# Nine weight areas loaded in order of use, two gather buffers, an activation product in place

## The reference

```
def hier_moe(h, w_group, w_expert, w_gate, w_up, w_down):
    ...
    _, g_sel = lax.top_k(g_logit, 1)
    ...
    top_v, top_i = lax.top_k(e_sel, TOP_K_INNER)
    ...
    for g in range(N_GROUPS):
        hg = jax.nn.silu(jnp.einsum('td,edf->tef', t, w_gate[g])) * jnp.einsum('td,edf->tef', t, w_up[g])
        out = out + jnp.einsum('tef,efd->td', hg * comb[:, g, :, None], w_down[g])
```

## Time and profile before

| what | value |
|---|---|
| median of 3 runs | 1335.24 us (1334.73 to 1337.06) |
| profiled execution, its own time | 1332.0 us |
| its span | 1329.8 us |
| mean granted TensorE clock | 0.925 |
| TensorE busy | 1125.2 us (85%) |
| expert stage of layer 0, first gate-and-up product to last down product | 538.8 to 781.2 us |
| expert stage of layer 1, the same | 1057.5 to 1301.2 us |
| weights read per expert stage | 48 loads of 2048 KB |
| DMA rate in 600 to 770 us | 419 GB/s |

### The profile page before, as it was taken

One profiled execution on the slowest core, in us unless ns is written; L12 is line 12 of the kernel. 1 busy time (PEld: TensorE's weight loads), 2 busy tenths in 40 slices (PEclk: granted clock), 3 DMA queues, 4 the chain that ended last, 5 costly groups with the idle time before them and its releaser, 6 DMA issues.

```text
span 1329.8 us, 15315 instructions
## 1 busy us (share of the span) xinstructions
PE 1125.2 (85%) x6494; PEld 587.2 (44%) x6494; DVE 373.1 (28%) x854; ACT 246.4 (19%) x568; POOL 147.5 (11%) x135
## 2 busy tenths in 40 slices
PE   5999999999998996898777848997799599777871
PEld 3444444666897655333323314464345433223330
DVE  2511221234666423111101122019811311011114
ACT  4111211204301021111101112006611111011112
POOL 0000000143710000411110000000000221111000
PEclk9999999899999996898888888998899599888996
DMA  9210200000003535699999964015020699999955
GB/s 371 95 64 29 100 0 0 0 0 0 3 4 148 219 146 221 257 420 422 421 423 421 404 270 196 0 34 241 1 79 32 243 402 420 420 424 421 422 244 198
DMA packets 42235, 273.21 MB, mean 205 GB/s; under 512 B 8528, under 2 KB 9296, under 8 KB 21488
## 3 DMA queue, kind: packets, MB, share of 16 engines
q1 hardware_dynamic: 32368, 255.20, 46.8%
q0 software_dynamic: 9792, 16.94, 3.5%
HBM read 265.68 MB, written 23.21 MB: 217 GB/s over the span
## 4 chain that ended last, share of the span: by engine, by line
PE 62%; DMA 23%; DVE 8%; ACT 3%; issue 2%; SPq 0%; POOL 0%; DVEq 0%; POOLq 0%; ACTq 0%
DMA arena<-w_dn_dram 21%; PE bank L612 15%; PE bank L856 8%; PE bank L913 7%; PE bank L905 7%; PE bank L1030 5%; PE bank L692 4%; PE bank L653 2%; PE bank L660 2%; DVE arena L1747 2%; PE bank L596 1%; DVE arena L1717 1%; PE bank L944 1%; PE bank L555 1%; PE bank L847 1%
## 5 line engine op out<-in xcount | busy, mean ns | idle before, releaser
L905 PE MATMUL bank<-arena 128*64 128x512 f32 x1024 | 229.6, 601 | 1.7 <-ACT arena L1253 1.7
L913 PE MATMUL bank<-arena 128*64 128x512 f32 x512 | 140.0, 697 | 77.4 <-DMA arena<-w_dn_dram 70.4
L612 PE MATMUL bank<-arena 128*128 128x512 f32 x448 | 194.7, 594 | 0.9 <-ACT arena L1128 0.9
L905 PEld LDWEIGHTS bank<-arena 128*64 128x64 f32 x1024 | 81.5, 139 | 142.9 <-issue 140.2
L612 PEld LDWEIGHTS bank<-arena 128*128 128x128 f32 x448 | 84.8, 190 | 107.9 <-issue 106.8
L856 PE MATMUL bank<-arena 128*128 128x512 f32 x256 | 112.7, 595 | 0.7 <-ACT arena L1332 0.7
L913 PEld LDWEIGHTS bank<-arena 128*64 128x64 f32 x512 | 43.4, 159 | 152.7 <-issue 138.8
L1843 POOL DMA_INDIRECT arena<-h_dram,arena x32 | 32.7, 1022 | 437.2 <-DVE arena L1646 428.0
L1684 DVE COPY arena<-bank 128x512 f32<-128x512 f32 x32 | 22.1, 692 | 208.3 <-PE bank L913 208.3
L1847 POOL DMA_INDIRECT yk_dram<-arena x32 | 32.0, 999 | 398.2 <-DVE arena L1684 397.5
L1678 DVE TENSOR_TENSOR arena<-arena,bank 128x256 f32<-128x256 f32 x32 | 13.5, 421 | 215.3 <-ACT arena L1259 215.3
(11 more groups left out here) (234 smaller groups left out, 1163.4 us busy)
## 6 DMA issues: line engine op xcount, KB each, us to landing
arena<-w_gu_dram SPq DMA_DIRECT2D x52, 2048.0 KB, 28.3
arena<-w_dn_dram SPq DMA_DIRECT2D x32, 2048.0 KB, 26.5
arena<-w_in_dram SPq DMA_DIRECT2D x7, 2048.0 KB, 7.9
arena<-w_gu_dram SPq DMA_DIRECT2D x12, 1024.0 KB, 20.4
arena<-w_gu_dram SPq DMA_DIRECT2D x24, 512.0 KB, 25.2
arena<-w_out_dram SPq DMA_DIRECT2D x2, 4096.0 KB, 17.8
arena<-yk_dram SPq DMA_DIRECT2D x16, 512.0 KB, 6.9
arena<-w_qkv_dram SPq DMA_DIRECT2D x3, 2048.0 KB, 18.9
```

Source lines behind the costliest of these rows:

```text
L612: i = mm(pb[m % 4][:, :], wchunk[c % 3][:, k, (m % 4) * P:(m % 4 + 1) * P], HT[:, k, :], start=(k == 0), stop=(k == KT - 1))
L905: i = mm(out[cols, :], xT[:, k, cols], w(h, k), start=(k == 0), stop=(k == KT - 1))
L913: i = mm(pb[5 + c][cols, :], aT[:, f, cols], w[:, h, f, c * U:(c + 1) * U], start=(f == 0), stop=(f == 1))
```

## The change

It does five things.

- Down weights get a third area. Pair e uses set `e % 3` for its two gate and up pieces and its down weights, so there are nine areas. SP loads pair e+3's three pieces in order, each as soon as pair e's is read. Before the stage's first product all nine are loaded. The areas lie elsewhere: one gate-and-up piece of set 2 is now in four parts.
- The gather buffers `xg` go from four to two; a gather for pair e+2 waits until pair e is transposed, and the third and fourth gathers now stand between the table scatters.
- The product of silu and up is written over the silu (`act_h = sil`).
- The gain row for the norm behind the stage is loaded near the stage's end, not at its start. The first two attention projection pieces are loaded after the last down weights, once the down product of pair 13 is done.
- Between the layers, layer 1's first pair is loaded right after the last projection piece, and `wo[1]` waits until the query, key and value projections are done (`a_pm`), since it now lies where their weights were.

```diff
-        gu_piece = [[[(18 + 16 * j + 8 * c, 8)] for c in range(2)] for j in range(2)] + \
-                   [[[(78, 8)], [(74, 4), (92, 2), (98, 2)]]]
+        gu_piece = [[[(18, 8)], [(26, 8)]], [[(58, 8)], [(78, 8)]],
+                    [[(50, 8)], [(86, 3), (92, 1), (93, 1), (97, 3)]]]
...
-        dn = [units(50 + 8 * s, 8).rearrange("p (h f n) -> p h f n", h=2, f=FE // P) for s in range(2)]
+        dn = [units(a, 8).rearrange("p (h f n) -> p h f n", h=2, f=FE // P) for a in (34, 42, 70)]
...
-        xg = [units(66 + 2 * s, 2) for s in range(4)]
+        xg = [units(66 + 2 * s, 2) for s in range(2)]
...
-        act_h = [units(89)[:, 256 * s:256 * s + 256] for s in range(2)]
+        act_h = sil
...
-        def gu_turn(L, e):
-
-            j = (e + 2) % 3
-            return j, (NPAIR // 3 + (j == 2)) * L + e // 3 + 1
-
-        def dn_turn(L, e):
-
-            return (e + 1) % 2, NPAIR // 2 * L + e // 2 + 1
+        def turn_of(L, e):
+
+            j = e % 3
+            return j, len(range(j, NPAIR, 3)) * L + e // 3 + 1
...
-                sp.dma_start(GAIN[2 * L + 2], gains[2 * L + 2, :, :]).then_inc(ld_gain, 16)
+                load_down(L, 1)
+                load_gate_up(L, 2)
+                sp.wait_ge(s_tr, 8 * (2 * L + 2))
+                sp.wait_ge(r_hd, 16 * NT * (L + 1))
+                load_down(L, 2)
+
+                B = NPAIR * L
+                for e in range(NPAIR - 3):
+                    for c in range(2):
+                        sp.wait_ge(e_GU, 2 * (B + e) + 1 + c)
+                        load_gate_up(L, e + 3, (c,))
+                    sp.wait_ge(e_D, B + e + 1)
+                    load_down(L, e + 3)
                 if L == 0:
-                    load_gate_up(L, 0, (1,))
-                    load_gate_up(L, 2, (1,))
-                    load_down(L, 1)
-                else:
-                    load_gate_up(L, 0, (1,))
-                    load_gate_up(L, 2)
-
-                B = NPAIR * L
-                for e in range(NPAIR - 2):
-                    if e + 3 < NPAIR:
-                        for c in range(2):
-                            sp.wait_ge(e_GU, 2 * (B + e) + 1 + c)
-                            load_gate_up(L, e + 3, (c,))
-                    sp.wait_ge(e_D, B + e + 1)
-                    load_down(L, e + 2)
-                if L == 0:
+                    sp.wait_ge(e_D, NPAIR - 2)
                     for s in range(2):
                         sp.dma_start(aw[s], w_qkv[s, :, :, :]).then_inc(ld_wc[s], 16)
+                sp.wait_ge(e_GU, 2 * (B + NPAIR - 1))
+                sp.dma_start(GAIN[2 * L + 2], gains[2 * L + 2, :, :]).then_inc(ld_gain, 16)
...
             sp.wait_ge(c_o, 2)
+            load_gate_up(0, 0)
+            load_down(0, 0)
+            sp.wait_ge(o_n, NT)
             load_gate_up(0, 1)
-            load_gate_up(0, 2, (0,))
-            sp.wait_ge(o_n, NT)
-            load_down(0, 0)
-            load_gate_up(0, 0, (0,))
             moe_loads(0)
             sp.wait_ge(e_D, NPAIR)
             sp.dma_start(aw[2], w_qkv[2, :, :, :]).then_inc(ld_wc[2], 16)
+            sp.dma_start(negd, dconst[:, :].rearrange("p (b k) -> p b k", b=2)).then_inc(ld_dist, 16)
+            load_gate_up(1, 0)
+            load_down(1, 0)
+            sp.wait_ge(a_pm, 14)
             sp.dma_start(wo[1], w_out1[:, :, :]).then_inc(ld_wo, 16)
-            sp.dma_start(negd, dconst[:, :].rearrange("p (b k) -> p b k", b=2)).then_inc(ld_dist, 16)
-            sp.wait_ge(a_pm, 14)
-            load_gate_up(1, 1)
-            for e in range(2):
-                load_down(1, e)
+            load_gate_up(1, 1, (0,))
             sp.wait_ge(s_h, 3 * NT)
             routing_loads(1)
             sp.wait_ge(a_oc, 8)
-            load_gate_up(1, 0, (0,))
+            load_gate_up(1, 1, (1,))
             moe_loads(1)
...
+                def next_gather(e):
+                    pool.wait_ge(e_T, B + e - 1)
+                    gather(e, e % 2, gat_i[:, e:e + 1])
+
...
                 for e in range(NPAIR):
-                    if e + 4 < NPAIR:
-                        pool.wait_ge(e_T, B + e + 1)
-                        gather(e + 4, e % 4, gat_i[:, e + 4:e + 5])
+                    if 4 <= e + 3 < NPAIR:
+                        next_gather(e + 3)
```

More of the change, by code:

```diff
@@ L257, in trunk_program @@
         GAIN = [units(62, 2)] + [units(86, 2)] * 4
-        JUNK = [units(64, 2)] + [units(88, 2)] * 4
-        xg = [units(66 + 2 * s, 2) for s in range(4)]
+        JUNK = [units(64, 2)] + [units(89, 2)] * 4
+        xg = [units(66 + 2 * s, 2) for s in range(2)]
         xgT = [units(12 + 2 * s, 2).rearrange("p (k t) -> p k t", k=KT) for s in range(2)]
         yt = [units(8 + 2 * s, 2) for s in range(2)]
-        sil = [units(88)[:, 256 * s:256 * s + 256] for s in range(2)]
-        act_h = [units(89)[:, 256 * s:256 * s + 256] for s in range(2)]
+        sil = [units(89)[:, 256 * s:256 * s + 256] for s in range(2)]
+        act_h = sil
         actT = [units(90)[:, 256 * s:256 * s + 256].rearrange("p (j t) -> p j t", j=2) for s in range(2)]
@@ L279, in trunk_program @@
         GTEMP, BETA, GG, GC, KDS, KBS = range(6)
-        rt = units(94, 4)
+        rt = units(94, 3)
         lg = rt[:, 0:144].rearrange("p (t n) -> p t n", t=NT)
@@ L371, in trunk_program @@
         r_sc, r_hd = sem("ids_scattered"), sem("h_stored")
-        w_gs, w_ds = [sems(f"gate_up_loaded{j}_", 2) for j in range(3)], sems("down_loaded", 2)
-        def gu_turn(L, e):
-            j = (e + 2) % 3
-            return j, (NPAIR // 3 + (j == 2)) * L + e // 3 + 1
-        def dn_turn(L, e):
-            return (e + 1) % 2, NPAIR // 2 * L + e // 2 + 1
-        e_xg = sems("expert_gathered", 4)
+        w_gs, w_ds = [sems(f"gate_up_loaded{j}_", 2) for j in range(3)], sems("down_loaded", 3)
+        def turn_of(L, e):
+            j = e % 3
+            return j, len(range(j, NPAIR, 3)) * L + e // 3 + 1
+        e_xg = sems("expert_gathered", 2)
         e_T, e_xa, e_xd = sem("exp_transposed"), sem("exp_xT_a_copied"), sem("exp_xT_d_copied")
@@ L954, in gate_up @@
                     for c in range(2):
-                        b, turn = gu_turn(L, e)
+                        b, turn = turn_of(L, e)
                         pe.wait_ge(w_gs[b][c], 16 * len(gu_piece[b][c]) * turn)
@@ L971, in down @@
                         pe.wait_ge(e_yd, e + B)
-                    b, turn = dn_turn(L, e)
+                    b, turn = turn_of(L, e)
                     pe.wait_ge(w_ds[b], 16 * turn)
@@ L977, in moe @@
                 for e in range(NPAIR):
-                    gate_up(e, e % 4)
+                    gate_up(e, e % 2)
                     if e + 1 < NPAIR:
-                        transposes(e + 1, (e + 1) % 4)
-                    act_transposes(e, e % 4)
-                    down(e, e % 4)
+                        transposes(e + 1, (e + 1) % 2)
+                    act_transposes(e, e % 2)
+                    down(e, e % 2)
                     if e == 3:
@@ L1848, in scatter @@
                                           bounds_check=last_row, oob_is_err=False).then_inc(e_sc[j % 2], 16)
-                for j in range(4):
-                    gather(j, j, gat_i[:, j:j + 1])
+                def next_gather(e):
+                    pool.wait_ge(e_T, B + e - 1)
+                    gather(e, e % 2, gat_i[:, e:e + 1])
+                for e in range(2):
+                    gather(e, e, gat_i[:, e:e + 1])
                 pool.wait_ge(tab_init, 32)
```

29 lines of the change are left out of this document (15 added, 14 removed).

## The result

The changed kernel took 1320.07 us (median of 4 runs, 1317.84 to 1322.48), the kernel before on the same chip 1334.99 us (4 runs): a ratio of 0.9905, 95% interval 0.9882 to 0.9928. The forecast was 1317 us. The profiled execution had a span of 1319.6 us and a time of 1321.82 us at a mean clock of 0.941; before these were 1329.8, 1332.0 and 0.925.

The account below looks back on a forecast made before the run. DMA bytes were taken to set the expert stages' pace, 16.55 us a pair, so only the ends could gain: 7.7 us in layer 0 plus 10.7 in layer 1, 18.4 off 1335.2, gives 1317 us; bounds 1310 to 1329, range 1309 to 1328.

Parts of the forecast that it names:

- the two ends at which order can act: Expert stage's start (areas filled before the first release) and end (work behind the last weights); load order cannot change the pace between.
- sum of 18.4 us: Forecast gain of both layers together: 7.7 us in layer 0 and 10.7 us in layer 1.
- slot of 5.5: Time of one weight load in the full expert stage, 5.5 us, a pair's three loads taking 16.55 us.
- First gather: Stage start: the gather lands 0.2 us after the fuller queue empties, 1.9 us late in layer 0, 2.4 in layer 1.
- rival of a 7 us delay: Each stage's first gather waits 7 us, like gathers of the full stage, eating most of the gain: 1326 to 1332; chance 0.12.
- Ninth area: Stage start: one more load done before the first release, 39 instead of 40 follow, last weights land 5.5 us earlier per layer.
- Strict order: Stage end: pair 15's down weights land last, with only one down product behind them, taken as 4.5 us.
- End of layer 0: Two projection loads and the gain row (4.7 MB, 11.2 us) run against the last scatter, which lands at 778.4.
- Small edits: In the expert stages, two gather buffers for four and the product written in place were to cost nothing.
- Slower by the clock: Rival: after waits, each of a pair's three product bursts loses 2.9 us to half clock, 21.2 us a pair: 1381; chance 0.06.
- The waits vanish: Rival: loads stay ahead, both stages run at 12.5 us a pair, 70 us of waits go: about 1250; chance 0.03.

Follow-up runs that it names:

- changed again: The changed kernel without any edit, timed a second time: 1320.54 us, ratio 0.9907 to the kernel before.
- old order: Changed kernel, nine areas kept, but pair 14's down weights again issued behind pair 15's gate and up weights at each stage's end: 1333.08 us.
- projections behind the rows: Changed kernel with the first two attention projection loads issued after the read-back of the result rows: 1315.31 us.
- every piece split: Changed kernel with every gate-and-up piece loaded as four DMAs: 1325.88 us.
- new order alone: Kernel before, eight areas, with pair e+2's down weights issued ahead of pair e+3's gate and up weights from e = 6 on: 1321.66 us.
- the run with fewer bytes: Changed kernel loading only an eighth of each down-weight load from pair 3 on, so results are wrong: 1256.54 us, one run.
- small edits alone: Kernel before with two gather buffers, third and fourth gathers between the table scatters, and the product written over the silu: 1333.26 us.
- both moves: Changed kernel with the ninth load issued after the first gather lands and the two projection loads after the result rows' read-back: 1311.82 us, again 1313.40.

## Why the prediction was right, step by step

The bound, the two ends at which order can act, and the place of the new waits were as forecast: waits at gate and up pieces, from 648 us on (forecast 655), a pace of 16.5 us a pair, DMA share 1.01, one product behind the last weights, a last scatter over 4 us. The sum of 18.4 us was too large: the profiled span lost 10.2, the medians 12.5 to 15. That 1320.07 lies only 3 us above the forecast of 1317 is in part luck. In the traces 8 us of the sum are missing, and in the later runs 6: from their 1333.1 us for the kernel before, the same 18.4 us would have given 1314.7, against 1320.5. The terms:

| term | forecast, layers 0 and 1 | measured |
|---|---|---|
| first gather late | 1.9, 2.4 us | 3.0 (538.97 for 535.90), 3.5 (6.9 for 3.4) |
| refill: first issue to last weights | -4.9, -4.9 (a slot of 5.5, less 0.6) | -3.4 (222.3 for 225.7), -2.5 (222.8 for 225.3) |
| behind the last weights, to the last product's end | 4.5, 4.5 | 3.8, 5.5 |
| layer 0: last scatter lands behind the last weights | 11.4 | 11.8 |

- **First gather.** Mechanism right: it lands when the queue empties. In the four other kernels that were profiled with the whole ninth load ahead of both gathers (changed again, old order, projections behind the rows, every piece split) it landed 0.2 to 0.4 us behind that load in both layers too. Size off by 1.1 us in each layer: the queue emptied at 538.7 and not at 537.6, later than the load's 5.0 us less the gain row; why is open. The Trainium skill ("DMA: Bandwidth & Descriptors", section "Queues, rings and completion order") has DMA engines serve their queues in turn, packet by packet; by that alone the gather need not have waited for the queue to empty, and the traces show that it did (7.04 and 6.9 us for 4.10 and 3.4). The rival of a 7 us delay fell too.
- **Ninth area.** This is the term that was mis-sized most. I gave it a slot of 5.5 us less 0.6 for extra gathers. That counted one load less (2.10 MB) and took the other traffic as unchanged. The DMA queues from the first refill's issue to the last weights in layer 0 (packets, MB, share of 16 engines; q1 holds the plain loads, q0 the indirect transfers), after and then before, are

```profile
q1 hardware_dynamic: 10387, 84.76, 91.4%
q0 software_dynamic: 4096, 7.50, 8.9%
...
yk_dram<-arena POOLq DMA_INDIRECT x15, 10.0
arena<-h_dram,arena POOLq DMA_INDIRECT x13, 10.0
```

```profile
q1 hardware_dynamic: 10041, 86.22, 91.7%
q0 software_dynamic: 3872, 7.08, 8.2%
...
yk_dram<-arena POOLq DMA_INDIRECT x14, 10.3
arena<-h_dram,arena POOLq DMA_INDIRECT x12, 12.6
```

  The plain loads moved 1.46 MB less and not 2.10, because more of what stands behind the last weights in the queue moved before these had landed (2.97 MB for 2.33, by what is left when 39 and 40 weight loads are taken off). The gathers and scatters moved 0.42 MB more, with two more of them inside the refill. In layer 1 the same view (1063.1 to 1288.4 us before, 1062.4 to 1285.2 after) has 82.30 for 83.89 MB of plain loads and 7.63 for 7.14 of the others. There the gain row, of 0.52 MB, went from ahead of the stage to its end (issued at 1267.5, landed at 1286.3), and the forecast counted nothing for it there. Net, 1.04 and 1.10 MB less were moved, which at 420 GB/s is 2.5 and 2.6 us: by this estimate all of layer 1's 2.5 and most of layer 0's 3.4. In the traces the refills gave 5.9 us and the late gathers took 6.5 back; by the medians about 1 us was left, where 5.5 had been forecast (11.0 for two slots, less 4.3 for the gathers and 1.2 for the transfers). With the load out of the gather's way it was 4.7 us.
- **Strict order.** Right. The work behind the last weights shrank from 11.2 and 12.7 us to 3.8 and 5.5, 14.6 us together where 14.9 had been forecast. In whole kernels it was worth 11.0 us (the new order alone, with what it does to layer 0's last scatter in it) and 12.5 (the old order put back).
- **End of layer 0.** The number came out (11.8 us for 11.4), and the scatter did wait for the queue: it landed at 781.5, 0.2 us behind the gain row, the last of the loads ahead of it (issue, then landing):

```profile
L486 SPq DMA_DIRECT2D arena<-gains_dram x1: 328/328/328, 752.6 to 752.6; - x1
...
DMA to landing us min/median/max: 28.7/28.7/28.7
```

  But the working was not right, so the size was luck. The 11.2 us were 4.7 MB at the full rate. More than half of these had moved when the last weights landed at 769.7; behind that the engines moved 1.9 MB in 10 us, at 246 and 142 GB/s (last three numbers: granted clock, DMA share, GB/s):

```profile
770.00:775.00 5.00, 3.46 (x16) 1.04 (x13) 0.69 (x1) 0.90 (x2) 0.05 (x1) 1.00 0.60 246
775.00:780.00 5.00, 0.00 (x0) 0.00 (x0) 0.00 (x0) 0.98 (x1) 0.92 (x1) 0.77 0.36 142
```

  The slow end of the queue took the time, and not the bytes. That the projection loads cost about 3 us there is confirmed by moving them.
- **Small edits.** Nothing, as forecast.
- **Slower by the clock.** Fell as a loss, but not wholly. The granted clock over 600 to 770 us rose from 0.90 to 1.00, and in layer 0 every product that followed a wait for weights ran at 3.65 or 3.66 us a half. In layer 1 three of the 15 ran at 5.35 us, after 2.01, 2.50 and 1.21 us:

```profile
1231.36 5.35 PE L899 MATMUL bank<-arena 128*64 128x512 f32 x16 [2.50 <-DMA arena<-w_gu_dram]
```

  Two of them stood in a stage that waits for its loads anyway. The third is the last product, where its 1.7 us count: it is why 5.5 us passed behind layer 1's last weights. The Trainium skill ("TensorE: Matmul & The Clock Gate", section "HAM oscillation — how this bites in real kernels") describes a kernel in which every DMA wait, of some 3 to 5 us, sends the next burst off at half rate. The waits here were shorter, 0.5 to 2.8 us, and three of 34 had such an effect; so the loop that this rival took over for each burst did not come about.
- **The waits vanish.** Not with this change; the run with fewer bytes shows what it would take.

## What to carry to other kernels

Where a stage streams its weights at the DMA engines' full rate, count what work stands behind the last load to land: here one load two places too late at the end of each stage cost 11 to 12.5 us, while the bigger buffer gave about one in the changed kernel and nothing with the old order. The deeper prefetch paid only once the extra load no longer stood ahead of a small transfer that the stage's start waits for; issue it behind that. Bulk loads for the next stage did better behind the small last transfers of this one than ahead of them, by about 3 us here. Count, too, every transfer that a change moves into a stage whose pace is set by bytes, even a row of 0.5 MB.

## What the runs showed of the hardware

- Waits of one length did not always have one effect on the clock. The granted clock over 600 to 770 us was 0.90 with ten waits of up to 6.5 us (before), 0.91 with ten of up to 3.8 us (small edits alone), 0.96 with waits of up to 5.5 us (new order with eight areas), and 0.94 with one of 10.5 us and others of up to 2.7 (old order with nine areas). With waits of up to 2.8 us alone it was 1.00 in the changed kernel and 0.97 in the one with both moves. At the very end, the same wait of 1.21 us was followed by a last product of 5.35 us in three of these kernels' executions and of 3.65 us in two others.
- The queue does not drain at full rate to its end. After the last load of layer 1 is on its way, the DMA share falls over some 14 us, while the load takes 32 us from issue to landing (windows of the changed kernel; last: clock, DMA share, GB/s):

```profile
1271.00:1274.00 3.00, 2.14 (x10) 0.43 (x6) 0.69 (x1) 0.60 (x1) 0.00 (x0) 1.00 0.90 377
1274.00:1277.00 3.00, 2.77 (x14) 1.26 (x16) 0.00 (x0) 0.00 (x0) 0.97 (x1) 1.00 0.83 350
1277.00:1280.00 3.00, 1.82 (x11) 0.37 (x8) 0.00 (x0) 0.00 (x0) 0.00 (x0) 1.00 0.54 225
1280.00:1283.00 3.00, 2.71 (x14) 0.69 (x10) 0.00 (x0) 0.24 (x1) 0.00 (x0) 1.00 0.28 116
1283.00:1286.00 3.00, 1.14 (x6) 0.60 (x8) 0.42 (x1) 0.53 (x2) 0.00 (x0) 1.00 0.14 59
```

  The share is a mean over the 16 engines. It fits engines that are done while others still work on the last load, but this view does not tell them apart. The idle shares add up to 3 x (0.10 + 0.17 + 0.46 + 0.72) + 2.2 x 0.86 = 6.2 us, an estimate of how much earlier the last weights could land if the full rate held to the end. Why it doesn't, no run here tells.
- SP's issues can last long. In the changed kernel the loads of down weights at 556.47 took 0.33 us to issue, those at 619.41, 644.95 and 739.00 took 7.32, 7.91 and 3.44, and the last one of layer 1 4.04. By then the DMA engines had long been full. The chain that ended last passes through four of SP's issues, of 1.97 to 7.91 us, between 635.33 and 652.86 us; what they cost, no run here separates.
